# Retention values with tokens on partitions, and sliding-window attention with one score matmul per chunk

## What is computed

```python
# retention: 4 heads, dk = 64, dv = 128
scores = einsum('bcnhd,bcmhd->bchnm', qc, kc) * decay_in     # rope'd q and k
y = (inner + cross).reshape(B, S, H, dv)                     # scores @ v, all earlier chunks through R
y = head_rms(y) * silu(g)          # head_rms: y * rsqrt(mean(y*y over dv) + EPS), per token and head
# sliding-window attention: 8 query heads, 2 kv heads, hd = 64, window = this chunk of 64 and the one before
s = einsum('bcqhgd,bckhd->bchgqk', qc, kb);  p = softmax([s, sink])[..., :-1];  o = p @ vb
# HGRN2: o_t = S_t^T q_t, S_t = diag(f_t) S_{t-1} + (1-f_t) i_t^T, with lower-triangular A inside a block
```

## Time and profile before

| what | value |
|---|---|
| median of 3 runs | 991.19 us (989.63 to 991.42) |
| the profiled execution's own time | 991.44 us |
| its span, first to last instruction | 989.7 us |
| mean granted TensorE clock | 0.988 of full speed |
| PE busy, share of the span | 969.3 us, 98% |
| DVE, ACT, POOL busy | 574.1 us (58%), 396.5 us (40%), 34.5 us (3%) |
| chain that ended last, share of PE | 95% |
| DMA | 93.24 MB, mean 94 GB/s |

### The profile page before, as it was taken

One profiled execution on the slowest core, in us unless ns is written; L12 is line 12 of the kernel. 1 busy time (PEld: TensorE's weight loads), 2 busy tenths in 40 slices (PEclk: granted clock), 3 DMA queues, 4 the chain that ended last, 5 costly groups with the idle time before them and its releaser, 6 DMA issues.

```text
span 989.7 us, 12244 instructions
## 1 busy us (share of the span) xinstructions
PE 969.3 (98%) x4803; PEld 810.9 (82%) x4803; DVE 574.1 (58%) x658; ACT 396.5 (40%) x433; POOL 34.5 (3%) x27
## 2 busy tenths in 40 slices
PE   6999999999999999999999989999999999999996
PEld 5899889777788888888888968888888888888885
DVE  4877555554548654466545547787677677632322
ACT  6363223333643652233433445544444444422221
POOL 1000000200000000000021004100000000000000
PEclk8999999999999999999999999999999999999998
DMA  7414212122123244323323214334333432233322
GB/s 248 147 49 128 66 62 86 47 92 66 41 64 107 75 142 117 87 80 106 127 85 128 64 64 119 94 88 123 87 85 100 112 85 72 87 90 113 89 58 85
DMA packets 141080, 93.24 MB, mean 94 GB/s; under 512 B 4502, under 2 KB 138998, under 8 KB 140918
## 3 DMA queue, kind: packets, MB, share of 16 engines
q1 hardware_dynamic: 141046, 92.75, 31.4%
HBM read 90.64 MB, written 2.10 MB: 94 GB/s over the span
## 4 chain that ended last, share of the span: by engine, by line
PE 95%; DVE 2%; ACT 1%; DMA 1%; SPq 1%; issue 0%; DVEq 0%; ACTq 0%
PE ps L483 80%; PE ps L806 4%; PE ps L590 2%; PE ps L527 2%; PE ps L582 1%; PE ps L820 1%; DMA raw<-in_w_in 1%; PE ps L836 1%; PE ps L627 1%; PE ps L533 1%; PE ps L541 1%; PE ps L596 1%; ACT wH L975 0%; DVE hgF L1298 0%; DVE hgG L1461 0%
## 5 line engine op out<-in xcount | busy, mean ns | idle before, releaser
L483 PE MATMUL ps<-hH,wH 128*128 128x512 f32 x784 | 310.2, 396 | 1.8 <-DVE hL L1305 1.8
L483 PE MATMUL ps<-hL,wH 128*128 128x512 f32 x784 | 306.8, 391 | 0.0
L483 PE MATMUL ps<-hH,wL 128*128 128x512 f32 x784 | 306.6, 391 | 0.0
L1298 DVE TENSOR_TENSOR wL<-raw,wH 128x2048 fp32r<-128x2048 f32 (+3 forms) x94 | 190.4, 2026 | 124.1 <-ACT wH L975 124.1
L975 ACT ACTIVATE wH<-raw 128x2048 fp32r<-128x2048 f32 (+3 forms) x94 | 159.7, 1699 | 222.8 <-PE ps L483 219.8
L483 PEld LDWEIGHTS ps<-hH,wH 128*128 128x128 f32 x784 | 148.2, 189 | 35.5 <-DVE wL L1298 2.5
L483 PEld LDWEIGHTS ps<-hH,wL 128*128 128x128 f32 x784 | 148.1, 189 | 31.1
L483 PEld LDWEIGHTS ps<-hL,wH 128*128 128x128 f32 x784 | 148.2, 189 | 30.4 <-issue 0.2
L483 PE MATMUL ps<-actH,wH 128*128 128x512 f32 x176 | 69.1, 393 | 0.0
L483 PE MATMUL ps<-actH,wL 128*128 128x512 f32 x176 | 68.6, 390 | 0.0
L483 PE MATMUL ps<-actL,wH 128*128 128x512 f32 x176 | 68.5, 389 | 0.0
(11 more groups left out here) (275 smaller groups left out, 1280.6 us busy)
## 6 DMA issues: line engine op xcount, KB each, us to landing
raw<-in_w_in SPq DMA_DIRECT2D x58, 512.0 KB, 4.1
raw<-in_w_up SPq DMA_DIRECT2D x44, 512.0 KB, 4.5
raw<-in_w_branch SPq DMA_DIRECT2D x24, 256.0 KB, 4.3
raw<-in_w_down SPq DMA_DIRECT2D x16, 384.0 KB, 3.2
raw<-in_w_down SPq DMA_DIRECT2D x16, 320.0 KB, 3.7
raw<-in_w_out SPq DMA_DIRECT2D x8, 512.0 KB, 4.0
raw<-in_w_mkv SPq DMA_DIRECT2D x8, 512.0 KB, 4.4
xtok<-in_x SPq DMA_DIRECT2D x4, 512.0 KB, 6.1
```

What stands on the lines that cost most here:

```text
L483: last = pe.matmul(out_ap, a, b, start=start and k + m == 0, stop=stop and m == 2 and k == len(terms) - 1)
L1298: q.sig(dve.tensor_tensor(out_ap, a, b, op), sem)
```

## The change

HGRN2's level 2 is computed with 96 columns of weights and 64 streamed columns instead of 128 and 128, and DVE copies its two 32x32 blocks of each tile and head without a mask. Retention's values are computed with tokens on partitions (`r_values`): `att` is the weight and the values stream, 128 columns a matmul. The squares are then summed along rows by DVE (job 18), the root is taken from there (ACT job 19), DVE job 19 scales the rows, PE job 19 transposes the 16 blocks, and DVE job 20 multiplies with the gate out of PSUM. The 16 one-column matmuls, the 16 spreading matmuls and the multiplication `rY * rG` in job 19 go. In the attention every chunk but the first takes one score matmul for its 128 keys, and both `s_scores` and `s_values` change r with every matmul; `vb` gets its rows in the new order of keys. Some buffers change places (`rY`, `yaH`, `yaL`, `memtok`).

```diff
--- before.py
+++ after.py
@@ -238,10 +238,11 @@
         rG = at("rG", U[7], [P, H, S])
-        rY = at("rY", U[4], [P, H, S])
-        rsq = at("rsq", U[2], [P, H, S])
-        yaH = at("yaH", U[2], [P, KB, S], F32R)
-        yaL = at("yaL", U[3], [P, KB, S], F32R)
+        rYt = at("rYt", U[4], [P, NT, BR])
+        rsq = at("rsq", U[2], [P, NT, BR])
+        rY = at("rY", U[2], [P, H, S])
+        yaH = at("yaH", U[3], [P, KB, S], F32R)
+        yaL = at("yaL", U[4], [P, KB, S], F32R)
@@ -265,7 +266,7 @@
         ssqT = at("ssqT", U[4] + 4 * KIB, [P, S])
-        memtok = at("memtok", U[4], [P, MT, D])
+        memtok = at("memtok", U[2], [P, MT, D])
         mjunk = at("mjunk", U_AT + 8 * KIB, [P, D])
@@ -574,13 +575,21 @@
-                k1, q0 = (L, L) if li == 3 else (P, 0)
                 for i in range(NT):
                     pe.wait_ge(lev_taken, banks_free + i + 1)
+                    f = slice(P * i, P * i + P)
                     for h in range(H):
-                        w = P - q0
-                        last = pe.matmul(ps[0:k1, 4 + i, w * h:w * h + w], ks[:, h, P * i:P * i + k1],
-                                         hgQ[:, h, P * i + q0:P * i + P], start=True, stop=True)
+                        if li == 1:
+                            o, a, b = ps[:, 4 + i, P * h:P * h + P], ks[:, h, f], hgQ[:, h, f]
+                        elif li == 2:
+                            o = ps[0:96, 4 + i, L * h:L * h + L].rearrange("p (m t) -> p m t", m=2)
+                            a = ks[:, h, P * i:P * i + 96]
+                            b = hgQ[:, h, f].rearrange("p (m two t) -> p two m t", two=2, t=32)[:, 1]
+                        else:
+                            o = ps[0:L, 4 + i, L * h:L * h + L]
+                            a, b = ks[:, h, P * i:P * i + L], hgQ[:, h, P * i + L:P * i + P]
+                        last = pe.matmul(o, a, b, start=True, stop=True)
                     last.then_inc(lev_out, 1)
@@ -591,6 +600,15 @@
+            def r_values():
+                for i in range(NT):
+                    for h in range(H):
+                        for j in range(i + 1):
+                            last = pe.matmul(ps[:, 4 + i, P * h:P * h + P], att[j][:, h, P * (i - j):P * (i - j) + P],
+                                             rV[:, j, P * h:P * h + P], start=j == 0, stop=j == i)
+                    last.then_inc(r_o, 1)
             def r_scores(h, i, bank, c0):
@@ -599,33 +617,29 @@
-                for cp in range(2):
-                    for r in range(2):
-                        rows = slice(64 * r, 64 * r + 64)
-                        for cm in range(2):
-                            c = 4 * hf + 2 * cp + cm
-                            for v in range(2):
-                                q = sqc[rows, v, c].rearrange("p a t -> p (a t)")
-                                o = ps[:, 4 + 2 * cp + r, 256 * cm + 128 * v:256 * cm + 128 * v + 128]
-                                if cm:
-                                    last = pe.matmul(o, q, kd[rows, v, L * (c - 1):L * (c + 1)], start=True, stop=True)
-                                else:
-                                    odd = max(c - 1, 0)
-                                    pe.matmul(o[:, 0:L], q, kd[rows, v, L * c:L * c + L], start=True, stop=True)
-                                    last = pe.matmul(o[:, L:2 * L], q, kd[rows, v, L * odd:L * odd + L],
-                                                     start=True, stop=True)
+                for u in range(16):
+                    cp, cm, v, r = u // 8, u // 4 % 2, u // 2 % 2, u % 2
+                    c = 4 * hf + 2 * cp + cm
+                    rows = slice(64 * r, 64 * r + 64)
+                    q = sqc[rows, v, c].rearrange("p a t -> p (a t)")
+                    o = ps[:, 4 + 2 * cp + r, 256 * cm + 128 * v:256 * cm + 128 * v + 128]
+                    if c:
+                        last = pe.matmul(o, q, kd[rows, v, L * (c - 1):L * (c + 1)], start=True, stop=True)
+                    else:
+                        for half in range(2):
+                            pe.matmul(o[:, L * half:L * half + L], q, kd[rows, v, 0:L], start=True, stop=True)
                 last.then_inc(s_sc, 1)
                 for u in range(16):
-                    cp, r, cm, v = u // 8, u // 4 % 2, u // 2 % 2, u % 2
+                    cp, cm, v, r = u // 8, u // 4 % 2, u // 2 % 2, u % 2
                     c = 4 * hf + 2 * cp + cm
+                    w = 8 * cp + 4 * r + 2 * cm + v
                     band = sv[:, c // 2, :] if cm else vb[:, c // 2, :]
                     last = pe.matmul(o[:, :, L * (c % 4):L * (c % 4) + L], band[0:k, 64 * v:64 * v + 64],
-                                     sPT[0:k, u, :].rearrange("p (a t) -> p a t", a=2), start=True, stop=True)
+                                     sPT[0:k, w, :].rearrange("p (a t) -> p a t", a=2), start=True, stop=True)
                 last.then_inc(s_o, 1)
@@ -699,18 +713,17 @@
                     pe.wait_ge(r_att, 12)
-                    values(rV, r_o)
+                    r_values()
                 elif n == 18:
-                    pe.wait_ge(r_sqd, H)
-                    column_sums([[rsq[:, h, P * t:P * t + P]] for h in range(H) for t in range(NT)], 4, r_ms)
+                    pe.wait_ge(r_sqd, NT)
                     pe.wait_ge(taken, 17)
                 elif n == 19:
-                    pe.wait_ge(r_rs, 1)
+                    pe.wait_ge(r_yt, 1)
                     pe.wait_ge(sv_ready, 1)
                     for h in range(H):
-                        rows_of(statr[:, 4 * h:4 * h + 4], 4 + h, r_row)
+                        transposes([(ps[:, 4 + h, P * i:P * i + P], rYt[:, i, P * h:P * h + P]) for i in range(NT)],
+                                   r_T)
                 elif n == 20:
@@ -1067,20 +1080,21 @@
                 elif n == 18:
-                    for h in range(H):
-                        act.wait_ge(r_o, h + 1)
-                        do(rY[:, h, :], ps[:, 4 + h, :], ACT.Copy)
-                        do(rsq[:, h, :], ps[:, 4 + h, :], ACT.Square, r_sqd)
+                    for i in range(NT):
+                        act.wait_ge(r_o, i + 1)
+                        do(rYt[:, i, :], ps[:, 4 + i, :], ACT.Copy)
+                        do(rsq[:, i, :], ps[:, 4 + i, :], ACT.Square, r_sqd)
                 elif n == 19:
                     act.wait_ge(r_ms, 1)
-                    do(stat[:, :], ps[:, 4, 0:16], ACT.Sqrt, r_std, scale=1.0 / P, bias=eps[:, 0:1])
+                    do(stat[:, :], statr[:, :], ACT.Sqrt, r_std, scale=1.0 / P, bias=eps[:, 0:1])
                     act.wait_ge(s_rope, 1)
                     act.wait_ge(sv_ready, 1)
-                    do(vb[0:64, :, :], sv[0:64, :, :], ACT.Copy)
-                    do(vb[64:128, 1:NT, :], sv[64:128, 0:NT - 1, :], ACT.Copy, s_kd)
+                    do(vb[0:64, 0, :], sv[0:64, 0, :], ACT.Copy)
+                    do(vb[0:64, 1:NT, :], sv[64:128, 0:NT - 1, :], ACT.Copy)
+                    do(vb[64:128, 1:NT, :], sv[0:64, 1:NT, :], ACT.Copy, s_kd)
                 elif n == 20:
@@ -1416,6 +1430,12 @@
                     dve.wait_ge(lev_out, 4 * li + i + 1)
+                    if li == 2:
+                        for m in range(2):
+                            copy(att[i][L * m:L * m + 32, :, L * m + 32:L * m + 64],
+                                 ps[L * m:L * m + 32, 4 + i, 0:H * L].rearrange("p (h t) -> p h t", h=H)[
+                                     :, :, 32 * m:32 * m + 32], lev_taken if m else None)
+                        continue
                     if li == 3:
@@ -1556,18 +1576,20 @@
                         tt(sqc[:, v].rearrange("p c a t -> p a c t"), a, b, ALU.add, s_rope)
+                    dve.wait_ge(r_sqd, NT)
+                    q.sig(dve.reduce_sum(statr[:, :], rsq[:, :, :].rearrange("p i (h d) -> p (i h) d", h=H), AX_X), r_ms)
                 elif n == 19:
                     dve.wait_ge(r_std, 1)
-                    q.sig(dve.reciprocal(statr[:, :], stat[:, :]), r_rs)
+                    q.sig(dve.reciprocal(statr[:, :], stat[:, :]))
+                    q.settle()
+                    y = rYt[:, :, :].rearrange("p i (h d) -> p (i h) d", h=H)
+                    tt(y, y, statr[:, :].unsqueeze(2).to_broadcast([P, 16, P]), ALU.mult, r_yt)
+                elif n == 20:
                     dve.wait_ge(r_g, 1)
-                    dve.wait_ge(r_sqd, H)
-                    tt(rY[:, :, :], rY[:, :, :], rG[:, :, :], ALU.mult)
-                elif n == 20:
-                    dve.wait_ge(r_row, 4)
-                    q.settle()
-                    tt(rY[:, :, :], rY[:, :, :], ps[:, 4:8, :], ALU.mult, r_yf)
+                    dve.wait_ge(r_T, H)
+                    tt(rY[:, :, :], rG[:, :, :], ps[:, 4:8, :], ALU.mult, r_yf)
                 elif n == 21:
                     dve.wait_ge(r_hi, 1)
```

(4 more changed lines are left out.)

## The result

The changed kernel takes 978.54 us (median of 4 runs, 977.22 to 978.87) beside 990.84 us for the kernel before (median of 4): the ratio is 0.9884 with a 95% interval of 0.9858 to 0.9909. Run again on another occasion it took 978.41 us (6 runs) beside 989.68 (11 runs), 0.9894 (0.9870 to 0.9919). The forecast was 978.5.

What follows compares the result with a forecast made beforehand. PE was taken to bound the changed stretch (100 to 365 us), until another engine is late. Savings less added waits summed to -12.9 us, so 991.4 became 978.5 us; range 975.5 to 982.

Steps and rivals of the forecast that it cites:

- The largest term: Job 18 and its slot: 15.40 us becomes 8.62, -6.8: matmuls 4.5, transposes at full clock 0.5, slot 1.7.
- the upper bound: Job 17, retention's values: +0.2 us forecast, bounds 0 to +0.3.
- The handover of 0.3 us: Job 19: PE and DVE's scaled rows meet; +0.3 us for handover and first weight load (0 to +1).
- rival B: Clock falls once more, behind job 23's wait or job 19's transposes: 980.2 us, 981 with slow jobs; chance 0.22.
- rivals C and D: Scores and values: C, alternation pairs nothing, 984.0, chance 0.07; D, each change of r empties the array, 1004.7, chance 0.01.
- The wait at job 23: PE comes 4.2 us earlier to job 23 and waits there for ACT's last sPT: +1.9 us.
- rival A: Nothing is late; DVE's chain has unseen slack and job 23 doesn't wait: 976.6 us; chance 0.13.

Runs made afterwards that it cites:

- The parts alone: Kernel before with only retention's part: 983.06 us; only the attention's part: 987.96 us, again 986.94; only HGRN2's level 2: 990.89 us.
- yaL: Changed kernel with the subtraction yaL = rY - yaH moved from DVE to GpSimd: 979.68 us (6 runs).
- the order: Changed kernel with ACT taking slot 24's upper part and ybH earlier, and DVE taking ybL right behind the second half's softmax: 976.99 us (6 runs).

## Why the prediction was right

**The bound.** PE's path set the end in this stretch. What was taken from it up to job 19 came off the span in full; of the 4.3 us taken in the scores, 1.8 came back as a wait, as forecast. The parts alone give -8.3, -4.1 and -0.8 us in the chain, -13.2 together, the whole change -13.2.

**Job 18.** The largest term came from reading three things at once: the one-column matmuls, the transposes at half clock, and a slot of products 1.7 us too long. Putting the matmuls back returned all three (+6.7), while 128-column ones in their place cost their own length alone (+3.6). What the forecast did not say is that this was one of the kernel's executions and not all: without the fall the term is 12.2 - 8.65 = 3.5. Of the 4.5 us that the forecast gave to the matmuls themselves, 3.5 are theirs at full clock and 1.1 were the fall's, which cost 3.2 us in all. The profiled execution of before, at 991.44 us, lies near the slow end of its runs (985.9 to 992.8 over all occasions), which is why the medians differ by 11.3 to 12.3 us and not by 13.2. The absolute time came out since the changed kernel doesn't have that place. That 978.5 met the median of 978.54 so closely is luck: the terms were 0.3 us short of the profiled change, that execution lies 0.3 below the median, and the kernel's runs spread over 2.7 us.

**Jobs 7 and 17.** Weight columns between 64 and 128 did lie on the line between them: 0.084 us a record, forecast 0.087. That the streamed columns were halved as well was not tried apart. 80 records of 128 columns cost 0.1116 each, the upper bound: with the same streamed columns but 80 weight loads in place of 32, the weight loads are busy for all of job 17's 8.93 us (5.45 of 8.63 before), as in job 7 before, which has the same rate.

**Job 19.** The transposes took 1.75 us as in job 24. The handover of 0.3 us was not there: DVE's product ran from 272.74 to 275.03, and PE's first transpose started at 275.25. The Trainium skill ("TensorE: Matmul & The Clock Gate", Part 4) says that transposes do not count as activity as matmuls do; the slot behind these 16 took 8.21 us at clock 1.00 in the changed kernel, so no fall from them was seen here, and that cause of rival B did not come true.

**The alternation.** Pairs ran in every step: 0.062 us a record in job 21, 0.059 in job 25. No change of r cost anything, so rivals C and D fall. The rule of the Trainium skill ("TensorEngine Tiling (Array Packing)", Key Properties) that only a change of tiling mode drains, not of tile, agrees with that. Job 23, where 8 records use a tile of 64 rows before the rest use 128, took 0.21 us more than job 25; the forecast allowed 0.1 for it.

**What is late next.** The wait at job 23 was forecast at 1.9 us and measured 1.8, from one shift: PE 4.3 us earlier at job 23 (1.9 + 2.4), DVE's maximum over the first scores only 1.1 (3.35 us behind job 20's first record instead of 4.48). The runs show three things about it. It takes whatever the scores gain beyond some 2.5 us (the run without alternation); work beside its chain is not worth moving, a link in it is (yaL against the order); and in some executions a fall of the clock follows it, which costs 1.6 us more (job 23 and its slot 12.1 us instead of 10.5). Of eight profiled executions with a wait of 1.8 to 1.9 us there, three had a fall of the clock behind it, of three with 0.2 to 0.4 us none. So few cannot tell whether the shorter wait prevents the fall: none in three is no surprise at a rate of three in eight. Rival B got 0.22, which they do not contradict. The attention's part alone gained 1.9 and 3.1 us of 4.1 in the medians, and 5.6 with the wait cut, but part of that may be job 18's fall, as said above.

The other place of the same kind is the wait of 2.9 us in the cross-attention, which all kernels here share and none was built without. In 13 of the 14 profiled executions a fall followed it; the one without it was 1.3 to 1.7 us shorter there. So this place can set two runs of one kernel about that far apart. What decides whether the clock falls, here and in job 23, stays open.

**The range.** Its low end has a small slip: rival A with level 2 at its lower bound is 976.6 - 0.8 = 975.8, not 975.5. Nothing hangs on it.

## What to carry to other kernels

Before adding up what a faster engine saves, follow the other engines' chain from the first thing that it consumes to the next wait, and take the difference of the two shifts as the new wait; then look in that chain for links that stand there only by the order of the program, since moving one of those gives the time back. Price a run of one-column matmuls, or an idle time of 2 to 3 us, by what the products behind it take too, and profile more than one execution before writing that down as a fixed cost. Do the same before reading a cause from two medians whose runs spread wider than they differ. A reordering that only speeds up an engine in front of a wait is worth next to nothing until the wait is gone (0.3 us of 1.5 here).

## What was not expected of the hardware

The granted clock does not fall in every execution of the same program: 16 one-column matmuls took 3.46 us with a slot of 8.20 behind them in two profiles, and 3.8 to 4.7 us with 9.8 to 10.6 in four. A wait of 2.9 us was followed by half clock in 13 of 14, one of 1.8 to 1.9 us in 3 of 8.

Without the one-column matmuls the spread is smaller, but the runs do not tell it apart cleanly. The kernel before has runs from 985.9 to 992.8 us; retention's part alone spreads over 2.2 us, the changed kernel over 2.7 over both occasions, the version with the other order over 1.8. Against it stand the version without alternation, which has neither those matmuls nor the long wait and spreads over 3.3 us, the one with yaL on GpSimd (4.2), and the attention's part with the other order, which still has the matmuls and spreads over 1.8.

With an elementwise operation of GpSimd in its first 0.3 us, one of DVE took 1.89 instead of 1.76 us, seen once.
